# First unit's weights in two transfers, fewer idle products, and small transfers held back

## The reference

```python
def first_block(x, w_in, ...):
    proj = jnp.einsum('bsd,de->bse', x, w_in[l])   # x: (1, 256, 2048), w_in: (2048, 7176)
    (q, k, v, g_att, fg, c_b, c_c, c_h, g_conv, p_u, g_pool) = jnp.split(proj, IN_SPLITS, axis=-1)
    ...   # forgetting attention, short convolution, pooling; w_out; layer_norm
def second_block(...):
    ...   # rmsnorm; gated linear attention; swiglu (2048 x 11264 and 5632 x 2048); gate; rmsnorm
```

## Time and profile before

| | us |
|---|---|
| median of the runs | 1668.05 |
| profiled execution, its own time | 1668.22 |
| its span, first to last instruction | 1666.5 |
| TensorE busy | 1654.7 |
| VectorE busy | 1027.7 |
| ScalarE busy | 805.6 |
| GpSimd busy | 54.2 |

### The profile page before, as it was taken

The page is one execution under the profiler, slowest core; times in us unless marked ns, Lnnn a source line. Parts: engine busy times, 40 slices in busy tenths (PEclk is TensorE's granted clock), DMA queues, the critical chain, the costliest instruction groups (busy, mean ns, idle before and its releaser), DMA issues.

```text
span 1666.5 us, 23048 instructions
## 1 busy us (share of the span) xinstructions
PE 1654.7 (99%) x8440; PEld 1370.7 (82%) x8440; DVE 1027.7 (62%) x1148; ACT 805.6 (48%) x977; POOL 54.2 (3%) x83
## 2 busy tenths in 40 slices
PE   9999999999999999999999999999999999999997
PEld 7888888888888888888888888888888888888886
DVE  5554475665787999665555645546556556465755
ACT  5535454443567656664544444344444443444653
POOL 7000000000010000000000000000000000000001
PEclk9999999999999999999999999999999999999999
DMA  8666655666576556547566656666666666665553
GB/s 274 178 188 182 188 163 165 226 226 211 156 245 178 172 178 179 171 152 240 183 189 190 194 188 189 196 189 188 190 189 192 188 191 194 189 187 192 174 193 128
DMA packets 159140, 315.95 MB, mean 190 GB/s; under 512 B 9728, under 2 KB 9728, under 8 KB 158176
## 3 DMA queue, kind: packets, MB, share of 16 engines
q1 hardware_dynamic: 157456, 304.12, 59.6%
q0 software_dynamic: 1616, 10.87, 1.8%
HBM read 310.77 MB, written 4.19 MB: 189 GB/s over the span
## 4 chain that ended last, share of the span: by engine, by line
PE 99%; issue 0%; DMA 0%; DVE 0%; ACT 0%; POOLq 0%; POOL 0%; SPq 0%; DVEq 0%
PE acc L596 31%; PE acc L598 31%; PE acc L597 31%; PE aux L612 2%; PE aux L771 1%; PE aux L665 0%; DMA w_raw<-in_w_in 0%; PE acc L630 0%; PE aux L652 0%; PE aux L790 0%; PE acc L633 0%; PE aux L788 0%; PE acc L636 0%; PE aux L789 0%; PE aux L777 0%
## 5 line engine op out<-in xcount | busy, mean ns | idle before, releaser
L1358 DVE TENSOR_TENSOR w_lo<-w_raw,w_hi 128x1024 fp32r<-128x1024 f32 x572 | 702.0, 1230 | 563.8 <-ACT w_hi L971 562.8
L971 ACT CAST w_hi<-w_raw 128x1024 fp32r<-128x1024 f32 x572 | 601.0, 1051 | 804.6 <-PE acc L598 782.0
L596 PE MATMUL acc<-w_hi,a_hi 128*128 128x512 f32 x1648 | 648.9, 394 | 0.0
L598 PE MATMUL acc<-w_hi,a_lo 128*128 128x512 f32 x1648 | 642.0, 390 | 0.0
L597 PE MATMUL acc<-w_lo,a_hi 128*128 128x512 f32 x1648 | 641.6, 389 | 0.0
L598 PEld LDWEIGHTS acc<-w_hi,a_lo 128*128 128x128 f32 x1648 | 309.3, 188 | 65.2
L596 PEld LDWEIGHTS acc<-w_hi,a_hi 128*128 128x128 f32 x1648 | 309.4, 188 | 62.8 <-issue 0.3
L597 PEld LDWEIGHTS acc<-w_lo,a_hi 128*128 128x128 f32 x1648 | 309.6, 188 | 62.0
L596 PE MATMUL acc<-w_hi,act_hi 128*128 128x512 f32 x320 | 124.6, 389 | 0.0
L598 PE MATMUL acc<-w_hi,act_lo 128*128 128x512 f32 x320 | 124.5, 389 | 0.0
L597 PE MATMUL acc<-w_lo,act_hi 128*128 128x512 f32 x320 | 124.5, 389 | 0.0
(11 more groups left out here) (255 smaller groups left out, 814.5 us busy)
## 6 DMA issues: line engine op xcount, KB each, us to landing
w_raw<-in_ffn_w_in SPq DMA_DIRECT2D x176, 512.0 KB, 3.6
w_raw<-in_w_in SPq DMA_DIRECT2D x112, 512.0 KB, 3.7
w_raw<-in_gla_w_in SPq DMA_DIRECT2D x96, 512.0 KB, 3.8
w_raw<-in_ffn_w_out SPq DMA_DIRECT2D x88, 512.0 KB, 3.7
w_raw<-in_w_out SPq DMA_DIRECT2D x32, 512.0 KB, 4.6
w_raw<-in_gla_w_out SPq DMA_DIRECT2D x32, 512.0 KB, 3.8
w_raw<-in_ple_w_gate SPq DMA_DIRECT2D x32, 512.0 KB, 3.9
x_raw<-in_x_cols SPq DMA_DIRECT2D x8, 256.0 KB, 6.8
```

The costliest lines, as they stand in the source:

```text
L596: pe.matmul(banks[t][:], hi[:, k + c, tok], wh, start=st, stop=False)
L598: mm = pe.matmul(banks[t][:], lo[:, k + c, tok], wh, start=False, stop=en)
L971: nc.scalar.copy(w_hi[u % RING][:], w_raw[u % RING][:]).then_inc(hi_done, 1)
L1358: nc.vector.tensor_tensor(w_lo[u % RING][:], w_raw[u % RING][:], w_hi[u % RING][:], ALU.subtract).then_inc(lo_done, 1)
```

## The change

Unit 0's weights come in two transfers of one chunk each, with a semaphore for the first (`first_in`) beside that of the ring. ScalarE casts each chunk by itself. TensorE has a `first_unit` of its own in which chunk 0's products with `a_hi` and `a_lo` come before chunk 1 is waited for. `IDLE` goes from 14 to 9. GpSimd waits for x's fourth piece (`x_in[3]`) before it issues `fg_raw`; everything behind that in its queue moves with it.

```diff
-IDLE = 14
+IDLE = 9
@@ SyncE
             for c in range(RING):
                 sp.dma_start(x_raw[:, 2 * c:2 * c + 2, :], x_cols[:, 2 * c:2 * c + 2, :]).then_inc(x_in[c], 16)
-                load(U_IN + c, rows(w_in[0], c * xw, slice(COLS1[0], COLS1[0] + N)))
+                if c == 0:
+                    for k, done in enumerate((first_in, landed[0])):
+                        sp.dma_start(w_raw[0][:, k, :], w_in[0][k * P:(k + 1) * P, COLS1[0]:COLS1[0] + N]).then_inc(done, 16)
+                else:
+                    load(U_IN + c, rows(w_in[0], c * xw, slice(COLS1[0], COLS1[0] + N)))
@@ GpSimd
+            pool.wait_ge(x_in[RING - 1], 16)
             pool.dma_start(fg_raw[:], fg_cols).then_inc(fg_in, 16)
@@ TensorE
+            def first_unit():
+                banks = panel_banks(P_IN)
+                tiles = [(t, slice(t * P, (t + 1) * P)) for t in range(TT)]
+                pe.wait_ge(x_hi_done, 1)
+                pe.wait_ge(first_hi, 1)
+                for t, tok in tiles:
+                    pe.matmul(banks[t][:], a_hi[:, 0, tok], w_hi[0][:, 0, :], start=True, stop=False)
+                pe.wait_ge(x_lo_done, 1)
+                for t, tok in tiles:
+                    pe.matmul(banks[t][:], a_lo[:, 0, tok], w_hi[0][:, 0, :], start=False, stop=False)
+                pe.wait_ge(hi_done, 1)
+                for a in (a_hi, a_lo):
+                    for t, tok in tiles:
+                        pe.matmul(banks[t][:], a[:, 1, tok], w_hi[0][:, 1, :], start=False, stop=False)
+                pe.wait_ge(lo_done, 1)
+                for c in range(UNIT):
+                    for t, tok in tiles:
+                        mm = pe.matmul(banks[t][:], a_hi[:, c, tok], w_lo[0][:, c, :], start=False, stop=False)
+                mm.then_inc(unit_used, 1)
@@ early_unit
-                    pe.matmul(banks[t][:], a_hi[:, k + c, tok], w_hi[u][:, c, :], start=k + c == 0, stop=False)
+                    pe.matmul(banks[t][:], a_hi[:, k + c, tok], w_hi[u][:, c, :], start=False, stop=False)
@@ after still_products()
-            for u in range(RING):
+            first_unit()
+            for u in range(1, RING):
                 early_unit(u)
@@ ScalarE, in the loop over x's pieces
-                if c < RING:
+                if c == 0:
+                    for k, (there, done) in enumerate(((first_in, first_hi), (landed[0], hi_done))):
+                        act.wait_ge(there, 16)
+                        nc.scalar.copy(w_hi[0][:, k, :], w_raw[0][:, k, :]).then_inc(done, 1)
+                elif c < RING:
                     high(c)
@@ VectorE, low()
+                if u == 0:
+                    dve.wait_ge(first_hi, 1)
```

More of the change, by code:

```diff
@@ L341, in block_kernel @@
         still_set = sem("still_set")
+        first_in, first_hi = sem("first_in"), sem("first_hi")
         x_lo_done, p_lo_done = sem("x_lo_done"), sem("p_lo_done")
```

## The result

The changed kernel takes 1670.61 us (median of 18 runs, 1670.04 to 1672.74) where the kernel before takes 1667.97 beside it (18 runs, 1667.63 to 1668.17): ratio 1.0017, 95% interval 1.0011 to 1.0024. It is 2.6 us slower, less than the 0.2% that the prediction called no change, but clear of the noise, and more than twice the 1.1 us forecast. Its runs also spread over 2.7 us, those of before over 0.5. The profiled execution took 1672.74 us (span 1671.0), 4.5 us more than that of before. Three executions of 2806, 3029 and 5975 us (two of the kernel before beside experiments 5 to 8, one of experiment 2) are left out of all that follows.

What follows compares the result with a forecast made beforehand. TensorE's own unbroken work bounds the kernel, busy 1654.7 of 1666.5 us. Start +0.8 gained, wait for `fg_raw` -1.35 and VectorE beside `sel` -0.45 take the profiled 1668.2 to 1669.2, median 1669.1, range 1667.0 to 1670.8.

Steps and rivals of the forecast that it cites:

- no change: Whole kernel: a difference within 0.2%, 3.3 us, counts as the same; chance 0.95.
- the start's gain: TensorE's start: unit 1 begins at 9.3 and not 10.08, 0.8 us gained, which doesn't reach the end.
- The wait for `fg_raw`: ScalarE before unit 4's cast: `fg_raw` lands at 16.05, unit 4 starts at 18.8, a new stall of 1.35 us.
- the forecast's own case: Whole kernel: `fg_raw` lands late and the kernel is slower by +0.3 to +2 us; chance 0.65.
- the two clock cases: TensorE's clock lost early: three microseconds or more, chance 0.04; a short loss, up to +2.5, chance 0.03.
- First unit: Unit 0 in two transfers: first half lands at 5.1, first product at 5.85, 1.4 us earlier; unit 1 at 9.3.
- What the hold frees: DMA between units 1 and 2: 0.95 us freed, x's fourth piece lands at 10.8; worth nothing beyond the 0.8.
- rival (a): ScalarE before unit 4's cast: `fg_raw` lands in time, total 1667.3 to 1667.6 us; chance 0.26.
- VectorE beside `sel`: Unit 4's and 5's preparation beside GpSimd's selects: one hit of 0.85 on unit 5 expected, -0.45 in the sum.
- Rival (b): TensorE's first unit: gaps drop the clock to 1.2 GHz, 0.43 us per product for 0.227; chance 0.04 for three microseconds or more.
- Five idle products "worth nothing by themselves": TensorE's idle products, 14 to 9: no gain alone, they only let real work begin before 6.20 us.
- The forecast's own sum: Whole kernel: start +0.8 gained, `fg_raw` wait -1.35, VectorE beside `sel` -0.45; profiled execution from 1668.2 to 1669.2 us.

Runs made afterwards that it cites:

- experiment 5: Changed kernel with 12 more idle products ahead of unit 4, in the gap where TensorE waits for its weights: 1670.26 us.
- experiment 6: Changed kernel with 14 idle products in place of 9: 1670.20 us.
- experiment 7: Changed kernel without the hold and with 14 idle products, so only the first unit in two transfers is left: 1667.98 us.
- experiment 8: Changed kernel, hold kept, with the casts of `fg_raw` on ScalarE and VectorE moved from turn 4 to the end of turn 7: 1668.06 us.
- experiment 2: Kernel before with only GpSimd's wait for x's fourth piece added: 1669.82 us.
- experiment 4: Changed kernel with GpSimd's constants up to `sel` built ahead of the hold and the transfers behind it: 1669.75 us.
- experiment 10: Changed kernel with GpSimd's hold on x's third piece in place of its fourth: 1668.45 us.
- experiment 1: Changed kernel without GpSimd's wait for x's fourth piece; halves and nine idle products stay: 1668.49 us.
- experiment 11: Kernel before with 9 idle products in place of 14, nothing else changed: 1668.76 us.
- experiment 3: Changed kernel with `fg_raw` issued ahead of the hold; `b_f`, `vec` and the constants stay behind it: 1668.26 us.

## Why the prediction was wrong

Its direction and its chain were right: the start's gain is lost on the wait for `fg_raw`, which ends last. The sizes were not. The wait for `fg_raw`, priced at 1.35 us, was a gap of 1.8 to 3.1 us in the traces of the changed kernel and of experiments 2, 4 and 6, and the clock behind it was priced at nothing. The measured 1670.61 still lies inside the range of 1667.0 to 1670.8; but the loss of 2.6 us lies beyond the forecast's own case (up to +2) and between the two clock cases (up to +2.5, and three or more), which had 0.03 and 0.04. By its own steps:

- *First unit.* Unit 0 at 5.85 forecast, 5.45 measured: the first half landed by 4.69 and not at 5.1, near the lower bound (4.4 to 4.9 in the ten traces with halves). Unit 1 at 9.3, measured 9.34. As forecast, neither reaches the end; in experiment 7, without the hold, the time is that of before as well.
- *What the hold frees.* The 0.95 us between units 1 and 2 was put down to GpSimd's transfers. With those gone the two are still 10.63 - 8.15 = 2.48 apart, not 2.03: only 0.5 was theirs. So x's fourth piece landed at 11.3, not 10.8.
- *The wait for `fg_raw`: the term that was mis-sized.* Forecast: issue 10.85, flight 5.2, landing 16.05. Measured: 11.57 (0.5 from the step above, 0.2 from GpSimd's wake-up of 0.29), flight 5.8, landing 17.3. So unit 4's `low` started at 18.63 and not at 17.45, which is 1.2 of the 2.1 us by which unit 4 was misplaced (20.92 for 18.8). In the traces of experiments 2, 4, 5 and 6, with the same hold, `fg_raw` landed at 16.9 to 17.3 as well. The Trainium skill ("DMA: Bandwidth & Descriptors", section "Anatomy of one DMA — SWDGE (gpsimd) path") puts such a transfer at 2.0 us and bytes/436 GB/s, an estimate of 2.15 us for 64 KB, which rival (a) named; no run here shows it, the shortest flight of `fg_raw` being 3.7 us (experiment 7).
- *VectorE beside `sel`.* One hit of 0.85 was expected behind unit 4's `low`, in unit 5's preparation, and 0.45 of it was charged. It fell on `low` itself (2.14 for 1.23) in the changed kernel's trace, in full: the rest of the 2.1. The excess, 0.91, vanishes in experiment 4, in which the selects are done before. The Trainium skill ("SBUF — State Buffer", section "Who interferes with whom") says that a VectorE operation with two on-chip inputs contends with a GpSimd operation that reads the buffer; these traces agree. In the traces of experiments 2, 5, 6 and 10 the excess fell on `fg_two` (1.18 for 0.33) and cost nothing. How many of the untraced runs it strikes on `low` isn't known.
- *The clock.* Rival (b) had the mechanism and the price per product (0.2 us), but looked for it in the first unit's short gaps. It came in the gap that the forecast itself had predicted, before unit 4, which at 3.1 us is three times the harmless one of the earlier trace rows. The forecast opened a gap of 1.35 and priced only its length. Eight slow products cost 1.6 us in the traced run; in the median filling the gap saved 0.4 (experiment 5), which is not clear of the noise. Seven of the changed kernel's 18 runs lie at 1671.1 or above; five of these have a mean granted clock of 0.997, and all the lower ones have 0.998 or 0.999.
- *Five idle products "worth nothing by themselves".* Doubtful by about 0.7 us (experiments 1 and 7; alone in the kernel before, 0.8, experiment 11), with an interval on each that is wider than that. With nine of them the first real products ran at the lower clock in six traces (experiments 1, 3, 4, 5, 8 and 10), but unit 1 waited 0.3 to 0.75 us for its weights in each, so no trace shows a cost. The cause of the 0.7 stays open.

In the medians: the hold alone +2.0 (experiment 2, unit 4 at 19.67, 1.4 late in its trace), the whole change +2.6. The 0.6 between them is less than the interval of either, and its split is not shown. The forecast's own sum with the late start of `low` put in gives unit 4 at 20.0, 1.8 later than before: by estimate 1670.0 in place of the 1668.2 traced before, which is where the changed kernel's runs begin (1670.04). That they go up from there to 1672.74 fits runs in which the slow products (up to 1.6), the longer `low` (0.9), both or neither come on top; only single runs were traced, so the shares are not known.

## What to carry to other kernels

When a transfer is held back, look for the first instruction that waits for it on every engine that takes its work in order, and set landing against that place, with the flight time measured while the DMA engines are full and the wake-up of the issuing engine; here moving the use too cost nothing that shows (experiment 8), and moving the transfer alone cost 2 us (experiment 2). Before an earlier start is paid for, ask which landing the second and third unit hang on. Price a forecast gap in TensorE's work twice: its length, and the clock behind it.

## What the runs showed of the hardware

- When TensorE rises to 2.4 GHz after it starts differs between executions of nearly the same start: 14 idle products took 4.93 us in one trace, and 4.75, 5.67 and 5.73 in those of experiments 7, 6 and 2.
- At the start the profile's granted clock reads 1.00 even where the idle products are 0.43 apart (before, 1.3 to 4.7 us), so there the spacing alone tells the level.
- Gaps of 1.74 and 1.77 us (experiments 11 and 2) left full pace behind them; gaps of 1.90, 2.05 and 3.14 (experiments 6, 4 and the changed kernel) were followed by about eight products 0.43 apart, at a granted clock of 0.50. The first pair differs from the second by little, and the same three kernels also have runs without that loss, by their times; what decides it is not shown.
- A transfer of 64 KB issued from GpSimd took 5.4 to 5.8 us to land when it was issued at 9.5 to 11.9 us, with the DMA engines full. Issued at 1.8 us it took 5.2 and 4.9 us beside a whole first unit (before, experiment 11), and 3.7 to 4.0 beside one in halves (experiments 1, 3 and 7).
- A first unit in two transfers had its first half there at 4.4 to 4.9 us and its second at 5.2 to 6.0 (ten traces), while the single transfer landed at 5.6, 5.8 and 6.05 (experiments 2 and 11, before). The first half is sooner in every trace, the whole unit in most.
